# One block for projections, values and prompt attention, an earlier query split, hidden stores on SyncE, and a re-ordered gate tail in a one-layer decoder step

## The reference

```
u = rms(h); [q_f, k_f, v_f | q_d, k_d, v_d | f_logit] = u @ w_in
A: 8 heads: softmax(q k / 8 + sum of log sigmoid(f_logit + b_f)), causal      "forgetting attention"
B: 8 heads: three dilated windows with a relative bias, merged                "dilated attention"
h = h + [rms(o_A) | rms(o_B)] @ w_out
# product-key experts: 8 heads, 2 x 128 sub keys, the 16 best of 128*128 = 16384 experts
q = (rms(h) @ w_query).reshape(T, 8, 256)
s1, s2 = q[..., :128] @ keys1, q[..., 128:] @ keys2
top16 of the sums of top16(s1) and top16(s2) -> eidx, g = softmax(top)
hid = u_tab[eidx] . rms(h);  a = g * gelu(hid);  h = h + sum a * v_tab[eidx]
y = rms(h)
```

## Time and profile before

| | before |
|---|---|
| runs | 1828.43, 1829.7, 1831.84 us (median 1829.7) |
| the profiled execution: its time, its span | 1833.72 us, 1832.2 us |
| mean granted TensorE clock | 0.963 |
| PE busy | 1700.7 us (93%), 9914 matmuls |
| DVE busy | 1401.1 us (76%) |
| ACT busy | 771.0 us (42%) |
| POOL busy | 586.4 us (32%) |
| DMA | 470.82 MB, 257 GB/s over the span |

### The profile page before, as it was taken

One profiled execution on the slowest core, in us unless ns is written; L12 is line 12 of the kernel. 1 busy time (PEld: TensorE's weight loads), 2 busy tenths in 40 slices (PEclk: granted clock), 3 DMA queues, 4 the chain that ended last, 5 costly groups with the idle time before them and its releaser, 6 DMA issues.

```text
span 1832.2 us, 30280 instructions
## 1 busy us (share of the span) xinstructions
PE 1700.7 (93%) x9914; PEld 1496.8 (82%) x9914; DVE 1401.1 (76%) x3184; ACT 771.0 (42%) x1194; POOL 586.4 (32%) x515
## 2 busy tenths in 40 slices
PE   5997898698799999998998999998899999999997
PEld 3997744348699999998998999997788888888885
DVE  3234247624549999987997999997899999999998
ACT  3222034402344443335776767774333333333334
POOL 0010180000144454465433333432433333333331
PEclk8998889899799999999999999999999999999999
DMA  3342271153243333349998999999999999999994
GB/s 114 99 163 109 88 229 53 34 215 133 65 140 128 118 113 117 114 140 371 387 370 309 379 366 365 392 397 383 357 383 384 383 386 388 384 383 383 386 388 184
DMA packets 195263, 470.82 MB, mean 257 GB/s; under 512 B 17970, under 2 KB 100530, under 8 KB 192606
## 3 DMA queue, kind: packets, MB, share of 16 engines
q1 hardware_dynamic: 124062, 240.30, 37.3%
q0 software_dynamic: 50944, 178.96, 25.8%
q10 hardware_dynamic: 20160, 50.34, 7.1%
HBM read 411.97 MB, written 61.32 MB: 258 GB/s over the span
## 4 chain that ended last, share of the span: by engine, by line
DVE 28%; DMA 26%; PE 9%; issue 6%; ACT 3%; DVEq 0%; SPq 0%; ACTq 0%; POOL 0%; POOLq 0%
DMA vw<-in_v_experts 23%; DVE gathered L1407 3%; DVE og L1865 3%; PE hp L226 2%; DVE ulo L1889 2%; PE hp L227 2%; PE hp L228 2%; DVE vlo L1759 2%; ACT vhi L1755 2%; PE ggp L1809 2%; DVE vw L1407 2%; DMA gathered<-in_u_rows,idx_row 1%; DVE eq L1672 1%; DVE sc L1624 1%; DVE X L1631 1%
## 5 line engine op out<-in xcount | busy, mean ns | idle before, releaser
L226 PE MATMUL hp<-mid_hi,uhi 128*128 128x384 f32 x1024 | 359.7, 351 | 30.6 <-DVE ulo L1889 25.9
L227 PE MATMUL hp<-mid_lo,uhi 128*128 128x384 f32 x1024 | 348.3, 340 | 0.0
L228 PE MATMUL hp<-mid_hi,ulo 128*128 128x384 f32 x1024 | 347.3, 339 | 0.0
L226 PE MATMUL va<-vhi,ahi 128*128 128x512 f32 x768 | 299.0, 389 | 0.0
L228 PE MATMUL va<-vhi,alo 128*128 128x512 f32 x768 | 298.9, 389 | 0.0
L227 PE MATMUL va<-vlo,ahi 128*128 128x512 f32 x768 | 298.9, 389 | 0.0
L1747 POOL DMA_INDIRECT gathered<-in_v_experts,idx_row x160 | 188.3, 1177 | 334.2 <-DVEq L2189 277.7
L226 PEld LDWEIGHTS hp<-mid_hi,uhi 128*128 128x128 f32 x1024 | 195.8, 191 | 37.2 <-DVE ulo L1889 29.4
L1321 ACT ACTIVATE uhi<-uw 128x1024 fp32r<-128x1024 f32 x128 | 135.7, 1060 | 166.5 <-PE hp L228 115.8
L1755 ACT ACTIVATE vhi<-vw 128x1024 fp32r<-128x1024 f32 x128 | 134.7, 1053 | 157.5 <-DMA vw<-in_v_experts 155.2
L227 PEld LDWEIGHTS hp<-mid_lo,uhi 128*128 128x128 f32 x1024 | 195.7, 191 | 0.0
(11 more groups left out here) (335 smaller groups left out, 3396.4 us busy)
## 6 DMA issues: line engine op xcount, KB each, us to landing
uw<-in_u_experts SPq DMA_DIRECT2D x128, 512.0 KB, 6.0
vw<-in_v_experts SPq DMA_DIRECT2D x128, 512.0 KB, 10.5
hidden_values<-gelu_out ACTq DMA_DIRECT2D x128, 192.0 KB, 5.4
gate_matrix<-gst ACTq DMA_DIRECT2D x12, 2048.0 KB, 11.6
hd<-hidden_values SPq DMA_DIRECT2D x16, 768.0 KB, 9.4
gt<-gate_matrix SPq DMA_DIRECT2D x16, 768.0 KB, 13.5
uw<-hidden_values SPq DMA_DIRECT2D x16, 768.0 KB, 9.4
uw<-gate_matrix SPq DMA_DIRECT2D x16, 768.0 KB, 13.3
```

The lines of the kernel that those rows point to most:

```text
L226: nc.tensor.matmul(out, a_hi, b_hi, start=first, stop=False)
L227: nc.tensor.matmul(out, a_hi, b_lo, start=False, stop=False)
L228: return nc.tensor.matmul(out, a_lo, b_hi, start=False, stop=last)
```

## The change

It has four parts.

1. **One block.** The blocks of projections, values and prompt attention become one. Each engine runs its three functions (`project_on_*`, `values_on_*`, `attend_on_*`) in a row, with waits where a buffer is reused. The barrier behind the values goes, and so does the clear there (its semaphores are cleared behind the out-projection). The loop of the value products is unrolled. `turn_k` of the last pair moves behind the second value tile, its copy on DVE (`keep_k`) behind the forget chain. The turned logits are made at chunk 2 instead of at the end. `causal` now uses a buffer of the attention, and is loaded early; `g_out` no longer stands ahead of the scores.
2. **Early query split.** The two first `qwhi`/`qwlo` are made in the out-projection, on ACT behind its weight splits and on DVE behind `add_to_h(3, 0)`. The first four `u_experts` loads are issued there too.
3. **Hidden stores on SP.** In the gate stage's turns SP issues the stores to `hidden_values`, each one behind the next `u_fetch`; in the tail ACT still issues them.
4. **Tail.** The row products behind the six `ulo` splits are 3, 1, 1, 2, 3, 5 in place of 3, 3, 3, 3, 3, 0. The work on the first four value tiles stands behind all the splits, tile by tile (`hd`, `vlo`, `alo`), with `coef` ahead of the fourth; ACT rounds `vhi` two tiles later.

The diff, cut to its core:

```diff
+            def on_tensor(pe, between):
+                for chunk in range(w_tiles):
+                    pe.wait_ge(lo_done, chunk + 1)
+                    for t in range(TT):
+                        between(pe, chunk, t)
+                        pe.wait_ge(out_done, chunk * TT + t + 1)
...
                 product(NH - 1, 1)
-                turn_k(NH - 1)
...
-            @block.sync
-            def _(sp):
+            def values_on_sync(sp):
+                v_loads(sp)
                 sp.wait_ge(f_dve, 10)
+                sp.dma_start(cum_dram, cum[:]).then_inc(cum_out, 16)
                 sp.dma_start(logf_dram, logf[:]).then_inc(f_out, 16)
...
+                nc.vector.tensor_scalar(onesr[:], ident[:], 0.0, 1.0, ALU.mult, ALU.add).then_inc(const_ev, 1)
+                keep_k(dve, NH - 1)
...
+                def between(pe, chunk, t):
+                    if (chunk, t) == (0, 0):
+                        pe.wait_ge(ev_done, 2 * NH + 1)
+                    if (chunk, t) == (0, 2):
+                        turn_k(pe, NH - 1)
+                    if (chunk, t) == (0, 4):
+                        pe.wait_ge(f_act, 1)
+                    if (chunk, t) == (2, 0):
+                        turn_logits(pe)
...
-        nc.clear_and_free_semaphores(brief_sems)
-        nc.all_engine_barrier()
...
+            @block.tensor
+            def _(pe):
+                project_on_tensor(pe)
+                values_on_tensor(pe)
+                attend_on_tensor(pe)
...
+                for u in range(2):
+                    act.wait_ge(w_q_loaded[u], 16)
+                    nc.scalar.activation(q_hi[:, u], w_q[:, u], ACT.Copy).then_inc(q_split, 1)
...
                 add_to_h(CHUNKS - 1, 0)
+                for u in range(2):
+                    dve.wait_ge(q_split, u + 1)
+                    nc.vector.tensor_tensor(q_lo[:, u], w_q[:, u], q_hi[:, u].bitcast(F32), ALU.subtract)
...
+        def store_hidden(sp, m, i):
+            sp.wait_ge(gelu_done, m + 3)
+            sp.dma_start(gelu_dram[m], ge[:, i]).then_inc(ge_stored[i], 16)
...
+        TAIL_DOTS = (3, 4, 5, 7, 10, 15)
...
+            done = 0
             for e in range(GX - 2):
                 split_lo(NK - GX + e + 2, e % 2, (e + 2) % UR)
-                for t in range(3 * e, min(3 * e + 3, LAST_DOTS)):
+                upto = TAIL_DOTS[e]
+                for t in range(done, upto):
...
                 weigh(dve, c, 0)
-            for c in range(GT):
+                rest_of_v(dve, c, c)
                 rest_of_a(dve, c, c, 0)
...
                 for i in range(GTI):
                     u_fetch(sp, G0 + GTI * j + i + UR, slot(half, i))
+                    if i:
+                        store_hidden(sp, G0 + GTI * j + i - 1, (i - 1) % 2)
+                store_hidden(sp, G0 + GTI * j + GTI - 1, (GTI - 1) % 2)
```

More of the change, by code:

```diff
@@ L93, in build @@
         ident = sb(ctx, "ident", [P, P])
+        with ExitStack() as forget:
+            gz, ga, ge, gu, gl, gd, gw = (sb(forget, "g" + n, [NH, NT]) for n in ("z", "a", "e", "u", "l", "d", "w"))
+            logf = sb(forget, "logf", [NH, NT])
+            cum = sb(forget, "cum", [NH, SEQ])
+            lf = sb(forget, "lf", [P, TT, NH])
         mid_hi = sb(persistent, "mid_hi", [P, KD, NT], F32R)
@@ L457, in _, with keep_k, turn_k, project_on_vector @@
                 turn(NH - 1, True)
-            @block.vector
-            def _(dve):
+            def keep_k(dve, m):
+                dve.wait_ge(kt_done, m + 2)
+                dve.wait_ge(kn_free, m + 1)
+                nc.vector.tensor_copy(kn[:, 0:TT - 1], kp[:, 0:TT - 1])
+                nc.vector.tensor_copy(kn[:NS, TT - 1], kp[:NS, TT - 1]).then_inc(kn_done, 1)
+            def turn_k(pe, m):
+                pe.wait_ge(ev_done, 2 * m + 4)
+                pe.wait_ge(kn_done, m + 1)
+                for t in range(TT):
+                    r = rows(t)
+                    last = nc.tensor.transpose(kp[:r, t, :], kz[:, t * P:t * P + r], ident[:])
+                last.then_inc(kt_done, 1)
+            def project_on_vector(dve):
                 dve.sem_inc(lo_done, 2)
@@ new lines, in values_on_tensor, with turn_logits @@
+            def values_on_tensor(pe):
+                def between(pe, chunk, t):
[7 more added lines that the diff above has]
+                        turn_logits(pe)
+                def turn_logits(pe):
+                    pe.wait_ge(f_dve, 10)
+                    for t in range(TT - 1):
+                        nc.tensor.transpose(lp[:, TT + t], cum[:, t * P:(t + 1) * P], ident[:NH, :NH])
+                    for t in range(TT):
+                        r = rows(t)
+                        last = nc.tensor.transpose(lp[:r, t], logf[:, t * P:t * P + r], ident[:NH, :NH])
+                    last.then_inc(f_mm, 1)
+                v_products(pe, between)
@@ L1173, in build @@
         keys_loaded = sem("q_c")
+        q_hi = sb(early, "qwhi", [P, 2, KD, P], F32R)
+        q_lo = sb(early, "qwlo", [P, 2, KD, P], F32R)
+        u_load = [sem(f"u_load{i}") for i in range(UR)]
         x2r_spread = sem("x2r_spread")
@@ L1341, in hidden_gelu @@
             nc.scalar.activation(ge[:, i], hp[i][:, :TD], ACT.Gelu).then_inc(gelu_done, 1)
+            if not store:
+                return
             act.wait_ge(gelu_done, m + 3)
```

247 lines of the change are left out of this document (117 added, 130 removed).

## The result

| | before | changed |
|---|---|---|
| median | 1829.07 us (1828.02 to 1831.84) | 1812.38 us (1809.69 to 1814.75) |
| ratio | | 0.9903, interval 0.9881 to 0.9925 |
| span of the profiled execution | 1832.2 us | 1813.2 us |
| chain that ended last | DVE 28%, DMA 26%, PE 9% | PE 40%, DVE 25%, DMA 3% |

The account below looks back on a forecast made before the run. No single engine was taken to set the end (DVE 28%, DMA 26%, PE 9% of the chain). Terms -17.9 - 8.9 - 4.8 - 2 - 2 = -35.6 gave 1798.1 from the profiled 1833.7, 1794.1 us as median; range 1784 to 1808.

Parts of the forecast that it names:

- Part 1, meeting points: Key products to first scores: without the two PE gaps, scores start at 200.4 with a 1.8 us stall; -17.9 us.
- Part 2, the clock: Scores and first attention pairs: PE comes straight from value tiles, so its clock stays up; -8.9 us, bounds 0 and -10.1.
- Part 3, the route: Start of the route: with both query splits before the barrier the first product goes sooner; -4.8 us, bounds -4.8 and 0.
- Part 4, the stores: Gate stage turns: SP instead of ACT waits for `gelu_out` to issue hidden stores; -2 us, bounds 0 and -11.2.
- Part 5, the tail: Tail into value stage: PE there 9 us sooner, gain limited to unused transfer time; -2 us, bounds 0 and -3.6.
- stores late behind loads: Gate stage rival: stores queue behind loads on SP and land at some 11.8 us; +58, total 1854 us; chance 0.07.
- over 406 as a sign of a wrong mechanism: Gate stage turns: forecast at about 401 us; taking longer than 406 would show the prediction wrong in mechanism.
- no more than 4 us gained from the start of the tail to the end: Sign for the tail term: PE's wait of 6.57 gone, but at most 4 us gained from there to the end.
- the value stage follows PE: Value stage rival: PE, not transfers, sets the pace, so the tail gives 9 us and not 2; 1787 us; chance 0.12.

Follow-up runs that it names:

- the block alone: Changed kernel with query splits back in the route, stores on ACT and the old tail, early `u_experts` loads kept: 1807.21 us, 0.9877 of before.
- the load moved: Second gate load issued on SP ahead of the four `vw` refills: 1804.8 us on the changed kernel; 1826.27 on before with the new tail; 1801.52 with stores on ACT.
- the kernel with two matmuls of three: Changed kernel with one of three matmuls of each value product (high hidden by low expert values) left out: 1812.46 us.

## Why the prediction was wrong

The direction was right; the size was twice what came, and 1812.4 lies above the range.

- **Part 1, meeting points, -17.9: right.** First scores at 200.06 against a forecast of 200.4; stall 1.96 against 1.8.
- **Part 2, the clock, -8.9: right in mechanism, mis-sized.** In the profile of the change it took 7.6 us to the first exponential at a granted 1.00, as forecast. The Trainium skill (TensorE: Matmul & The Clock Gate, Part 1: The HAM clock gate) says that activity lifts the throttled state; the runs agree as to the two levels. But the 12.56 and 19.16 us of the earlier trace rows came from one execution in which the slow stretch lasted 21 us; three others with the same instructions there had 7, 7 and 13. By the medians the block was worth 21.3, which leaves 3.4; by the mean attention times of the profiles it is 4.7. The step that failed is the size of this term, read from one execution, and very likely a double count: the profiled execution stood 4.0 us above the median, and I took that off too, while its attention (135.3) was 4.1 longer than the mean of the four. The two profiled executions, of before and of the block alone, differ by 28.9 us, their medians by 21.3. One reading of the earlier trace rows was also incomplete: the matmuls directly behind the gap of 2.99 us were at full clock, but the next ones were not, as the row below shows (the same pair took 0.56 at full clock), so both gaps were followed by a low clock.

```profile
331.76 1.01 PE L791 MATMUL ST<-diag,onesr 128*128 128x384 f32 x2
```

- **Part 3, the route, -4.8:** 2.4 by the medians, 3.8 in the timeline. The first product comes 0.8 us behind the barrier and not at once, and from the last out-projection product to the barrier it now takes 15.9 us where it took 15.4. And the term was let through whole, while the entry of the gate stage took 2.7 us longer.
- **Part 4, the stores, -2:** between -4.0 and +3.3 in four pairs; no gain is shown. The rival (stores late behind loads) did not come true: the landing went from 6.2 to 7.8 us, not to 11. The turns were forecast at 401 us, with over 406 as a sign of a wrong mechanism. From the gelu of hidden tile 48 to that of tile 120 they took 411.6 us against 408.6 before, so 3.0 longer where 2 shorter were forecast, which puts them at that mark; the stores are not the cause, since in the kernels with the one block this stretch took 410.3 to 410.9 with the stores on ACT and 407.8 to 412.6 with them on SP.
- **Part 5, the tail, -2: wrong, +8.6, the largest part of the miss.** I asked what transfers the tail could free, and answered with the share of unused DMA time. The question that decided was which load PE would want next. `load_gates(sp, 1, 1)` stands on SP behind four refills; its issue follows the fourth `vlo`. Before, it had 1312.1 - 1289.5 = 22.6 us for a landing of 15.1 and for DVE's and ACT's work on it. Now the first product goes ahead of the fourth `vlo`, and it has 1282.2 - 1269.5 = 12.7 us for a landing of 18.7 and 3.8 us of that work. The prediction had this wait, and the low clock behind it, at nothing. I followed the moved `vlo` to PE, and to the `vw` loads, but not to what stands behind those on SP. The check that I named, "no more than 4 us gained from the start of the tail to the end", did not allow for a loss; 6.9 us were lost there.
- **The rival "the value stage follows PE":** PE did come to the stage some 8 us sooner (-33.0 against -24.9), but no run turned that into a gain of 9; with the load moved the new tail gave +1.0, -2.2 and -3.4 against the old one. And the stage is not bound by PE alone, as the kernel with two matmuls of three shows.

By the medians: block -21.3, queries -2.4, stores -0.2, tail +8.6, together -15.3, against a measured -16.7.

## What to carry to other kernels

When an engine's work is re-ordered, list every transfer whose issue waits for that work, and compare its issue and landing with the moment at which its reader will want it in the new order; a load that was in time by 2.6 us, counted to the operand made from it, became the wait that decided. Take a stretch at low clock from several executions before it becomes a term, and don't also subtract the distance of the profiled execution from the median. Where several resources read near full, a gain at a stage's start passes to its end only if everything that the stage's first tiles read has been issued in time.

## What the runs showed of the hardware

Behind a gap of 2.70 us on PE the granted clock stayed at 1.00 for the first 2 us of work and then was 0.50 for some 16.5 us; behind the gap of 6.4 to 6.5 of the kernels with before's blocks it was 0.50 from the first scores on, for 7, 7, 13 and 21 us in four profiles of the same instructions. And where the gate stage's loop jumps back DVE stood idle for 6.5 to 7.4 us in all fifteen profiles, with no releaser in fourteen of them, and PE with no releaser for 6.0 to 10.4 in the eleven with the one block and for 1.9 to 2.7 in the four without. A load of 768 KB took 12.0, 15.1 and 18.7 us from issue to landing in the kernel with the load moved, in before and in the changed kernel.
